# Dots moved between turns and engines, ScalarE making each fourth step's scaled one-hots, and attention's first turn reordered

## What is computed

```
q = (xt @ w_pq).reshape(T, H, 2, PEER_HALF)
s = einsum('thpd,hpkd->thpk', q, sub_keys)
s1, i1 = top_k(s[:, :, 0], 16);  s2, i2 = top_k(s[:, :, 1], 16)
idx, g  = best 16 of the 256 sums per head, and their softmax     # expert = i1 * 128 + i2
a = gelu(einsum('cd,ced->ce', x, u[idx])) * g
y = einsum('ce,ced->cd', a, v[idx]);  h = layer_norm(ALPHA * h + y)
```

## Time and profile before

| | |
|---|---|
| median of 3 runs | 2928.27 us (2920.92 to 2928.34) |
| the profiled execution | 2926.35 us, its span 2924.6 us |
| TensorE's granted clock, mean | 0.987 of full speed |
| busy share of the span | PE 96%, DVE 77%, ACT 39%, POOL 43% |
| borders of the turns of `experts_in` (first matmul of each) | 720.0, 839.5, 966.6, 1110.8, 1260.6, 1404.9, 1549.8, 1704.5 us; the last ends at 1857 us |

### The profile page before, as it was taken

How to read it: one execution, slowest core, us unless ns; L and a number is a source line. 1 busy time by engine, 2 the same in 40 slices (tenths; PEclk the granted TensorE clock), 3 DMA queues, 4 the chain that set the end, 5 groups by cost and what they waited for, 6 DMA issues and landing times. The chain is left out here.

```text
span 2924.6 us, 43095 instructions
## 1 busy us (share of the span) xinstructions
PE 2808.7 (96%) x15866; PEld 2519.9 (86%) x15866; DVE 2261.8 (77%) x4606; ACT 1146.1 (39%) x2153; POOL 1257.0 (43%) x915
## 2 busy tenths in 40 slices
PE   8997998999999999999999999999999999999997
PEld 7886886888989999999999989888888888888886
DVE  6115676466998998989896778488888888888887
ACT  3112232222333677677776667322222222222220
POOL 4123221000778655466666555134444444444441
PEclk9998999999999999999999999999999999999999
DMA  5224322222888878777878999899999999999991
GB/s 192 80 90 131 108 91 74 83 75 87 273 291 293 281 281 293 264 282 280 294 276 332 349 356 380 298 312 336 334 335 323 329 329 336 324 327 334 334 320 72
DMA packets 311485, 744.31 MB, mean 255 GB/s; under 512 B 22528, under 2 KB 136448, under 8 KB 308096
## 3 DMA queue, kind: packets, MB, share of 16 engines
q0 software_dynamic: 92160, 335.59, 31.9%
q1 hardware_dynamic: 190976, 307.68, 31.6%
q10 hardware_dynamic: 28160, 98.58, 8.5%
HBM read 623.26 MB, written 118.49 MB: 254 GB/s over the span
## 5 line engine op out<-in xcount | busy, mean ns | idle before, releaser
L1656 PE MATMUL y_ps<-v_hi,a_hi 128*128 128x512 f32 x1536 | 598.4, 390 | 6.2 <-DVE a_lo L1801 6.2
L1657 PE MATMUL y_ps<-v_lo,a_hi 128*128 128x512 f32 x1536 | 598.1, 389 | 0.0
L1658 PE MATMUL y_ps<-v_hi,a_lo 128*128 128x512 f32 x1536 | 598.0, 389 | 0.0
L890 POOL TENSOR_TENSOR u_lo<-u_raw,u_hi 128x1024 fp32r<-128x1024 f32 x128 | 308.0, 2406 | 517.8 <-ACT u_hi L886 517.3
L1233 PE MATMUL z_first<-hT_hi,u_hi 128*128 128x384 f32 x1024 | 353.9, 346 | 16.4 <-POOL u_lo L890 13.3
L1656 PEld LDWEIGHTS y_ps<-v_hi,a_hi 128*128 128x128 f32 x1536 | 288.6, 188 | 66.4 <-DVE a_lo L1801 6.4
L1234 PE MATMUL z_first<-hT_lo,u_hi 128*128 128x384 f32 x1024 | 345.5, 337 | 0.0
L1235 PE MATMUL z_first<-hT_hi,u_lo 128*128 128x384 f32 x1024 | 345.1, 337 | 0.0
L1658 PEld LDWEIGHTS y_ps<-v_hi,a_lo 128*128 128x128 f32 x1536 | 288.7, 188 | 60.2
L1657 PEld LDWEIGHTS y_ps<-v_lo,a_hi 128*128 128x128 f32 x1536 | 288.7, 188 | 59.8
L1233 PE MATMUL z_rest<-hT_hi,u_hi 128*128 128x256 f32 x1024 | 297.4, 290 | 1.0 <-ACT z_sb L1311 1.0
(11 more groups left out here) (232 smaller groups left out, 6140.1 us busy)
## 6 DMA issues: line engine op xcount, KB each, us to landing
u_raw<-in_uT SPq DMA_DIRECT2D x128, 512.0 KB, 5.0
room<-in_v SPq DMA_DIRECT2D x126, 512.0 KB, 7.2
z<-z_sb ACTq DMA_DIRECT2D x128, 320.0 KB, 6.1
gates<-late ACTq DMA_DIRECT2D x12, 2048.0 KB, 10.2
gates<-g_sb ACTq DMA_DIRECT2D x12, 2048.0 KB, 10.9
late<-gates SPq DMA_DIRECT2D x16, 1536.0 KB, 19.0
room<-gates SPq DMA_DIRECT2D x15, 1536.0 KB, 18.4
room<-z SPq DMA_DIRECT2D x16, 1280.0 KB, 8.2
```

What stands on the lines that cost most here:

```text
L890: self.nc.gpsimd.tensor_tensor(self.u_lo[e][:], self.u_raw[e][:], self.u_hi[e][:].bitcast(F32), ALU.subtract).then_inc(self.u_lo_in[e], 1)
L1656: nc.tensor.matmul(o, ah, v_hi[p][:, i, c], start=(opens(r, s) and i == 0), stop=False)
L1657: nc.tensor.matmul(o, ah, v_lo[p][:, i, c], start=False, stop=False)
L1658: last = nc.tensor.matmul(o, al, v_hi[p][:, i, c], start=False, stop=(closes(r, s) and i == GROUP - 1))
```

## The change

- Rows per turn: 34, 40, 34, 34, 34, 34, 62, 48 become 34, 40, 40, 40, 40, 40, 50, 36 (320 in all, as before). GpSimd and ScalarE take three rows in ten where they took one in five; the rule holds for the first six turns and, within each block of 128 rows, for rows 3 to 103.
- In turns 2 to 6, for each fourth gate step (`by_act`), VectorE makes only the one-hots of the second index. ScalarE makes the scaled one-hots of the first by itself: the distance `|iT - iota|` (Abs, four instructions), a wait for its own semaphore, and `Relu(gT - gT * distance)` (four instructions), which is `gT` where the distance is 0 and 0 elsewhere. For that VectorE makes `minus_gT` once a block. TensorE waits for `hot_in` besides `hot_g_in`; VectorE waits for the last `hot_g_in` of the block before it overwrites `iT` and `gT`.
- `attend`, turn 0: GpSimd does its first four splits of `w_out` after `negs` instead of two before and two after; VectorE makes `yT_lo` before the copies for the next turn; and the wait for the LayerNorm's weights moves from the end of turn 0 (VectorE and GpSimd) to where VectorE first reads them.

```diff
@@ attend, GpSimd
                         if not back:
-                            split_wo(range(2))
                             pool.wait_ge(negs, 1)
-                            split_wo(range(2, 4))
+                            split_wo(range(4))
...
                             split_wo(range(4, KT))
-                            pool.wait_ge(norm_here, 48)
@@ attend, VectorE
+                def keep():
+                    nc.vector.tensor_copy(v_prev[:], pj[:, COLS - SKV:COLS])
+                    nc.vector.tensor_copy(skT[:, 0], skT[:, 1]).then_inc(kept, 1)
...
                     if back:
+                        v.wait_ge(norm_here, 48)
                         link(nc.vector.scalar_tensor_tensor(hr[:], hr[:], lmv[:, 0:1], ln_w[:], ALU.subtract, ALU.mult))
...
-                        nc.vector.tensor_copy(v_prev[:], pj[:, COLS - SKV:COLS])
-                        if not back:
-                            nc.vector.tensor_copy(masks[:, 0], masks[:, 1])
-                        nc.vector.tensor_copy(skT[:, 0], skT[:, 1]).then_inc(kept, 1)
+                        if back:
+                            keep()
... (hT_lo and yT_lo)
                     if not back:
-                        v.wait_ge(norm_here, 48)
+                        nc.vector.tensor_copy(masks[:, 0], masks[:, 1])
+                        keep()
@@ experts_in
-    PER_TURN = [34, 40, 34, 34, 34, 34, 62, 48]
+    PER_TURN = [34, 40, 40, 40, 40, 40, 50, 36]
+    SIGNED = DB - 1
...
         def by_pool(i):
-            return i < sum(PER_TURN[:6]) and i % 5 == 3 and 2 < i % (PH * TOPK) < 104
+            return i < sum(PER_TURN[:6]) and i % 10 in (3, 6, 9) and 2 < i % (PH * TOPK) < 104
...
+        def by_act(step):
+            return step // SLOTS < SIGNED and step % 4 == 3
@@ experts_in, TensorE, gates(step)
+                    pe.wait_ge(hot_in[g], step // 2 + 1)
                     pe.wait_ge(hot_g_in[g], step // 2 + 1)
@@ experts_in, ScalarE, scale_hot(step)
+                    if by_act(step):
+                        act.wait_ge(turned, step // SLOTS + 1)
+                        wait(act, g_done[g], step // 2)
+                        for t in range(4):
+                            i = t0 + t
+                            last = nc.scalar.activation(hot[g][:, 0, t], iota[:], ACT.Abs, scale=-1.0,
+                                                        bias=iT[:, 0, i:i + 1])
+                        last.then_inc(apart, 1)
+                        act.wait_ge(apart, SLOTS // 4 * (step // SLOTS) + step % SLOTS // 4 + 1)
+                        for t in range(4):
+                            i = t0 + t
+                            last = nc.scalar.activation(hot1_g[g][:, t], hot[g][:, 0, t], ACT.Relu,
+                                                        scale=minus_gT[:, i:i + 1], bias=gT[:, i:i + 1])
+                        last.then_inc(hot_g_in[g], 1)
+                        return
@@ experts_in, VectorE, make_hot(step)
-                    nc.vector.tensor_tensor(hot[g][:], bc(bc(iota_ps, 1, 4), 1, 2), bc(iT[:, :, t0:t0 + 4], 3, NK),
-                                            ALU.is_equal).then_inc(hot_in[g], 1)
+                    if by_act(step):
+                        nc.vector.tensor_tensor(hot[g][:, 1], bc(iota_ps, 1, 4), bc(iT[:, 1, t0:t0 + 4], 2, NK),
+                                                ALU.is_equal).then_inc(hot_in[g], 1)
+                    else:
+                        (as before)
@@ experts_in, VectorE, slot 1 of a gate turn
                             v.wait_ge(found_T, s - FIRST + 1)
+                            wait(v, hot_g_in[1], SLOTS // 2 * (s - FIRST))
                             nc.vector.tensor_copy(iT[:], g_ps[0][:, 0:2])
+                            nc.vector.tensor_scalar(minus_gT[:], g_ps[0][:, 2], -1.0, None, ALU.mult)
                             link(nc.vector.tensor_copy(gT[:], g_ps[0][:, 2]))
+                            nc.vector.engine_nop().then_inc(turned, 1)
```

More of the change, by code:

```diff
@@ L1092, in experts_in @@
             ahead, (2, P), (P,), (3, PH * TOPK), *[(2, 4, NK)] * 2, *[(4, NK)] * 2, (NK, GT))
+        minus_gT = sb("minus_gT", [P, P])
         hot, hot1_g, g_sb = rest[0:2], rest[2:4], [rest[4], sb("g_sb", [P, NK, GT])]
@@ L1109, in experts_in @@
         gaps, exps = sem("gaps"), sem("exps4")
-        found_in, found_T = sem("found_in"), sem("found_T")
+        found_in, found_T, turned, apart = sem("found_in"), sem("found_T"), sem("turned"), sem("apart")
         hot_in = [sem(f"hot_in{g}") for g in range(2)]
@@ L1421, in make_hot @@
                     wait(v, g_done[g], step // 2)
-                    nc.vector.tensor_tensor(hot[g][:], bc(bc(iota_ps, 1, 4), 1, 2), bc(iT[:, :, t0:t0 + 4], 3, NK),
-                                            ALU.is_equal).then_inc(hot_in[g], 1)
+                    if by_act(step):
+                        nc.vector.tensor_tensor(hot[g][:, 1], bc(iota_ps, 1, 4), bc(iT[:, 1, t0:t0 + 4], 2, NK),
+                                                ALU.is_equal).then_inc(hot_in[g], 1)
+                    else:
+                        nc.vector.tensor_tensor(hot[g][:], bc(bc(iota_ps, 1, 4), 1, 2), bc(iT[:, :, t0:t0 + 4], 3, NK),
+                                                ALU.is_equal).then_inc(hot_in[g], 1)
                 def dot(i):
```

## The result

The changed kernel takes 2941.29 us (median of 6 runs, 2938.72 to 2949.01) against 2926.47 us for the kernel before in the same job: ratio 1.0053 (95% interval 1.0043 to 1.0064), slower by about 15 us. Forecast were 2918 us and a range of 2906 to 2938 us; both missed, and so did the likeliest sign. The profiled execution has a span of 2939.0 us, 14.4 us more than before.

The account below looks back on a forecast made before the run. TensorE, busy 96% of the span, was taken as the bound, so only its gaps and slow-clock stretches could be won. Terms -1.3 + 4 - 1 - 7 - 5 = -10.3 us gave 2918 us, range 2906 to 2938 us.

Parts of the forecast that it names:

- (c): Turns 2 to 6, fourth steps by ScalarE: VectorE 4.3 us a turn less, ScalarE 13 more, tight in slots with two steps.
- (d): Turns 2 to 5, 34 to 40 dots each: VectorE still relieved on balance; with (c) -1 us (-9 to +9).
- the cover: ScalarE's idle time in turn 4 would absorb its added one-hot work and sums: 133 of 144 us busy.
- Rival 2: Turns 2 to 5: ScalarE's lateness in two-step slots costs 13 us, taking back later gains; 2928 us, chance 22%.
- (a): Attention's first turn: earlier `yT_lo` lets TensorE's projection start 1.3 us earlier, then bound by `wo_lo`; -1.3 us (0 to -3).
- (b): Turns 0 and 1: seven dots moved to GpSimd and ScalarE cost 6.2 us, VectorE's relief returns 2; +4 us (-8 to +25).
- Rival 3: Turns 0 and 1: each added row delays `u_lo` by full product and sum, +25 us; 2939 us, chance 16%.
- (e): Turns 6 and 7, 12 dots less each: fewer waits for late rows and one-hots, -7 and -5 us.
- The floor of 140 us: Turns 2 to 6: about 140 us a turn if TensorE never paused, from stretches without pauses.
- rival 4: ScalarE's new functions need another activation table, +10 us in each of five turns; 2968 us, chance 2%.
- the two signs set down for a wrong prediction: Turns 0 and 1 growing by more than 10 us, or turn 6 keeping its waits despite fewer rows.
- turns 2 to 5 within 3 us of before: Check set for turns 2 to 5, with VectorE a few us less busy and ScalarE some 18 us more.

Follow-up runs that it names:

- e4: Changed kernel with one row in five for GpSimd and ScalarE and no fourth steps by ScalarE; new rows per turn and attention order stay: 2921 us.
- e12: Kernel before with attention's new order alone (small additions of the change left in): ratio 0.9999.
- e9: e4 with six of VectorE's dots in each of turns 2 to 5 over 64 of 1024 columns, rows still gathered: 2904.04 us.
- e2: Changed kernel without fourth steps by ScalarE, three rows in ten kept: 14.2 us less than the changed kernel.
- e13: Changed kernel with the fourth steps that share a slot with another step (15 and 31) given back to VectorE: 2931.99 us.
- e14: Changed kernel with fourth steps 15 and 31 given back to VectorE and one row in five instead of three in ten: 2914.03 us.
- e8: Changed kernel with GpSimd's products in turns 2 to 5 over 64 of 1024 columns: 2919.55 us.
- e17: Changed kernel with GpSimd's product ahead of `u_lo` from turn 2 on, all work kept: 2924.14 us.
- e7: Changed kernel with ScalarE's sums in turns 2 to 5 over 64 of 1024 columns: 2927.91 us.
- e3: Changed kernel with one row in five for GpSimd and ScalarE instead of three in ten, fourth steps kept: 2921.9 us.
- e11: Changed kernel with one row in five and rows per turn between old and new (38, 36, 38, 38, 54, 42 from turn 2): 2925.33 us.
- e10: Changed kernel with one row in five and the old rows per turn, fourth steps and attention order kept: 7.2 us more than e12 by the medians.
- e16: Changed kernel with each of ScalarE's sums one slot later in its order, all operations kept: 2951.71 us.

## Why the prediction was wrong

**The step that failed** is the sum of (c) and (d): "VectorE's relief against ScalarE's two-step slots, -1 us (-9 to +9)". It measured +27.4 us. The premise that broke first is the cover, "133 of 144 us. That fits on average": ScalarE's load fitted, its order did not (2 and 3 below). Three things are in it.

1. *The rows of (d).* The forecast netted the added dots against the fourth steps and the rows that three-in-ten takes off, and came out below nothing for VectorE. Alone they cost +18.7 us (e4 against e12), and e9 shows that they cost through VectorE's dots. The relief booked against them by three-in-ten did not come: with one in five turns 2 to 5 take 601.0 us, with three in ten, and 13 of VectorE's dots fewer, 600.6 (e4, e2). ScalarE's 13.4 us of waits for products in e2 may be what took it; no run has three-in-ten with the product first and no fourth steps, so that is not shown.
2. *The two-step slots of (c).* Rival 2 named them at 1.3 us a slot, 13 us in all, and I judged it less likely. e13 gives 9.3 us in ten slots. The forecast's argument against it, that other slots leave ScalarE 1 us, failed even with one in five, where the same slots hold 5.4 to 7.8 us (e14).
3. *The products in turns 2 to 5.* I gave them GpSimd's room (88.3 of 144.3 us) and ScalarE 5 us of sums, both by averages. ScalarE's 13 us and its 125.8 us in turn 4 came out as worked out; the quoted sentence counted load and left out that the sum waits in order for a product that stands behind `u_lo`, which waits for ScalarE. I had that loop for turns 0 and 1 and did not carry it on. In turn 4 before, the wait for products was 3.1 us; with one more row in ten it is 13.4 (e2), and with each fourth step 1.65 us longer on ScalarE there is no cover left for it. e8 and e17 show what the wait costs there, e2 and e7 that it needs ScalarE's longer order beside it.

The parts, by the turns of single executions: rows +18.7 (e12 to e4), three-in-ten -0.4 (to e2), fourth steps on both +10.0 (to the changed kernel): +28.3 us in turns 2 to 5.

**(a)** -1.3 us. The projection of attention's turn 1 does start 1.5 us earlier (290.53 against 292.05 in the earlier trace rows), but in this execution it was not bound by `wo_lo`, which was done at 289.53: TensorE was at 0.5 of full speed from 280 to 290.5 us and busy with the transposes until the projection began. That the number fits is luck here. In e12, whose transposes were done by 286.1, the mechanism is the predicted one, and the gain 2.35 us. The projection's first matmul in the changed kernel and in e12:

```profile
290.53 0.49 PE L462 MATMUL pa<-wo_hi,yT_hi 128*128 128x512 f32 x1
...
289.70 0.79 PE L462 MATMUL pa<-wo_hi,yT_hi 128*128 128x512 f32 x1 [3.67 <-POOL wo_lo L607]
```

In the whole kernel nothing of it can be told: e12 is at 0.9999, and `experts_in` starts anywhere from 714.6 to 720.3 us over these kernels, edit or not. Left open.

**(b)** +4 us; measured +8.7, all in turn 0. The sign and the mechanism were right, and the added waits for `u_lo` came out at the forecast's +6.2 us (13.3 to 19.5) over the two turns. The term was too small by half all the same: the 2 us that VectorE's relief was to give back did not come, and TensorE's busy time for the same matmuls grew by 3.0 us. By turns the average price of 0.9 us a row misled: turn 0 had paid 3.3 us for its seven rows, and there three more cost 8 us, while four more in turn 1 cost nothing. The clock does not explain turn 0: it was granted 0.99 before and 0.97 after, but 0.97 also in e12, whose turn 0 took 118.5 us. Rival 3 had the right place with too large a price; that its 2939 us lies next to the 2941 measured is chance, since its +25 us should have come in turns 0 and 1.

**(e)** -12 us; measured -18.9, and by the rows alone -21.1 (e4 against e12: -10.5 and -10.6). Mechanism right, term mis-sized: I took half of turn 6's excess back and most of it went, with 5.2 us left of the waits for one-hots. The floor of 140 us was itself too low: in e2 and e4 TensorE never pauses in turn 6 and takes 141.9 us, so turns 2, 4 and 5 before stood only 2 to 3 us above it and had little to give. The gain is no straight line in the rows: with fourth steps, 50, 54 and 62 rows take 144.3, 152.3 and 157.7 us (e3, e11, e10). The fourth steps gave nothing to it: turn 6 is 141.9 us without them and 144.3 with.

**The new functions' table (rival 4)** fell: nine loads on that line before and after.

That the fourth steps alone lose 5 us in turn 6 and about 9 in turns 2 to 5 is measured; the two-step slots account for part, the rest stays open. In turn 6 of e10 TensorE waits 10.1 us before gates against 6.8 in e12, once 2.9 us for VectorE's half of a fourth step.

Neither of the two signs set down for a wrong prediction came: turns 0 and 1 grew by 8.7 us, under the 10, and turn 6 lost most of its waits. The sign that did fail was "turns 2 to 5 within 3 us of before".

## What to carry to other kernels

Before work is moved to an idle engine, follow one instance in the timeline in that engine's own order: what it waits for, what stands ahead of that on the other engine, and whether the loop closes within one slot; idle time in a window (26 us in turn 4) does not show that. When two edits load the same engine, price them together, since each may fit a slot in which both don't. Here the product whose row had mostly landed belonged ahead of the `u_lo` that must wait for another engine (in turn 4 of e17 it waits 5.9 us for rows, and the turn is still shorter); moving the consumer later instead (e16) only handed the wait to whoever needs the buffer.

## What was not expected of the hardware

An accumulating operation has a second instruction behind it: the sum's ACTIVATE of 1.06 us is followed by a read of 0.185 us on ScalarE. The two overlap and so does what follows (ACTIVATE at 1369.27, read at 1370.23, the Gelu at 1370.32 in turn 4), so a sum holds ScalarE for some 1.05 us, about what the prediction took. A sum over 64 columns still took 0.26 us and a product over 64 columns 0.33 us, against 1.06 and 2.41 for 1024. In e16 TensorE was granted 0.97 in turn 4 instead of 0.99 in the changed kernel and 1.00 in e17, and was busy 147.0, 145.0 and 143.2 us with the same matmuls, so a part of what a wait costs comes behind it.
